# Loading a norm's rows later, and reordering the start of a norm's second tile, in a two-block transformer kernel

## What is computed

```python
x = layer_norm(ALPHA * x + 0.5 * swiglu(x, ffn1_gate[l], ffn1_up[l], ffn1_down[l]), ln1_g[l], ln1_b[l])
proj = x @ w_in[l]
(h_a, b_a, c_a, uv, q, kc, vc, ksl, vsl, kw, vw, gl) = jnp.split(proj, split_points, axis=-1)
y_a = short_conv(h_a, b_a, c_a, conv_w[l])
y_b = gmlp_spatial(uv, ...)
y_c = nsa_attention(q, kc, vc, ksl, vsl, kw, vw, gl, ...)
mix = jnp.concatenate([y_a, y_b, y_c], axis=-1) @ w_out[l]
x = layer_norm(ALPHA * x + mix, ln2_g[l], ln2_b[l])
x = layer_norm(ALPHA * x + 0.5 * swiglu(x, ffn2_gate[l], ffn2_up[l], ffn2_down[l]), ln3_g[l], ln3_b[l])
```

## Time and profile before

| | us |
|---|---|
| timed runs, median of 3 | 2010.58 (2009.91 to 2010.92) |
| profiled execution | 2009.22 |
| its span (first to last instruction) | 2007.4 |
| PE busy | 1980.2 |
| DVE busy | 1263.8 |
| ACT busy | 904.8 |
| POOL busy | 72.8 |

### The profile page before, as it was taken

The page is one execution under the profiler, slowest core; times in us unless marked ns, Lnnn a source line. Parts: engine busy times, 40 slices in busy tenths (PEclk is TensorE's granted clock), DMA queues, the critical chain, the costliest instruction groups (busy, mean ns, idle before and its releaser), DMA issues.

```text
span 2007.4 us, 31808 instructions
## 1 busy us (share of the span) xinstructions
PE 1980.2 (99%) x13856; PEld 1802.3 (90%) x13856; DVE 1263.8 (63%) x1790; ACT 904.8 (45%) x1188; POOL 72.8 (4%) x74
## 2 busy tenths in 40 slices
PE   8999999999999999999999999999999999999998
PEld 7888999999787999999899988799999998879997
DVE  6566666555656665655665567765566556776555
ACT  4445544444445444444344435444435444544442
POOL 0000001000100000100100010010010001001000
PEclk9999999999999999999999999999999999999999
DMA  7544556666543456686576655468657665546663
GB/s 288 168 146 142 181 197 195 206 206 190 175 163 132 166 175 199 189 251 189 168 217 190 187 153 158 106 191 244 189 170 225 186 189 150 149 107 193 189 189 105
DMA packets 421412, 361.84 MB, mean 180 GB/s; under 512 B 29392, under 2 KB 361496, under 8 KB 421272
## 3 DMA queue, kind: packets, MB, share of 16 engines
q1 hardware_dynamic: 421272, 359.80, 58.6%
HBM read 358.72 MB, written 1.05 MB: 179 GB/s over the span
## 4 chain that ended last, share of the span: by engine, by line
PE 89%; DVE 6%; ACT 2%; POOL 1%; DMA 1%; issue 1%; SPq 0%; DVEq 0%; ACTq 0%
PE ps L217 21%; PE ps L218 21%; PE ps L219 21%; PE ps L224 7%; PE ps L226 7%; PE ps L225 7%; PE ps L1488 2%; DVE hl L1997 2%; ACT hl L1776 1%; PE ps L1596 1%; DMA raw<-in_w_in 1%; POOL hl L1952 1%; PE ps L1630 1%; DVE xs L2057 0%; DVE small L2103 0%
## 5 line engine op out<-in xcount | busy, mean ns | idle before, releaser
L1997 DVE TENSOR_TENSOR hl<-raw,hl 128x1024 fp32r<-128x1024 f32 (+1 forms) x537 | 733.7, 1398 | 397.2 <-ACT hl L1776 395.9
L217 PE MATMUL ps<-xt,hl 128*128 128x256 f32 (+1 forms) x2672 | 755.2, 283 | 5.3 <-DVE hl L1997 5.3
L218 PE MATMUL ps<-xt,hl 128*128 128x256 f32 (+1 forms) x2672 | 746.9, 280 | 0.0
L219 PE MATMUL ps<-xt,hl 128*128 128x256 f32 (+1 forms) x2672 | 746.5, 279 | 0.0
L1776 ACT ACTIVATE hl<-raw 128x2048 fp32r<-128x2048 f32 (+1 forms) x323 | 612.3, 1900 | 224.1 <-PE ps L226 159.9
L217 PEld LDWEIGHTS ps<-xt,hl 128*128 128x128 f32 (+1 forms) x2672 | 501.7, 188 | 11.2 <-DVE hl L1997 5.7
L218 PEld LDWEIGHTS ps<-xt,hl 128*128 128x128 f32 (+1 forms) x2672 | 501.8, 188 | 3.1
L219 PEld LDWEIGHTS ps<-xt,hl 128*128 128x128 f32 (+1 forms) x2672 | 501.5, 188 | 0.2
L224 PE MATMUL ps<-hl,o 128*128 128x512 f32 x656 | 261.3, 398 | 0.0
L226 PE MATMUL ps<-hl,o 128*128 128x512 f32 x656 | 258.9, 395 | 0.0
L225 PE MATMUL ps<-hl,o 128*128 128x512 f32 x656 | 258.8, 394 | 0.0
(11 more groups left out here) (197 smaller groups left out, 1552.9 us busy)
## 6 DMA issues: line engine op xcount, KB each, us to landing
raw<-in_w_in SPq DMA_DIRECT2D x83, 1024.0 KB, 5.0
raw<-in_w_ffn_in SPq DMA_DIRECT2D x88, 512.0 KB, 5.1
raw<-in_ffn_gate SPq DMA_DIRECT2D x88, 512.0 KB, 3.9
raw<-in_ffn_up SPq DMA_DIRECT2D x88, 512.0 KB, 5.2
raw<-in_ffn_down SPq DMA_DIRECT2D x44, 1024.0 KB, 5.0
raw<-in_w_ffn_out SPq DMA_DIRECT2D x22, 1024.0 KB, 5.1
raw<-in_w_out SPq DMA_DIRECT2D x24, 512.0 KB, 4.8
raw<-in_w_branch_a SPq DMA_DIRECT2D x8, 1024.0 KB, 5.0
```

What stands on the lines that cost most here:

```text
L217: e.matmul(out, l[0], r[0], start=start, stop=False)
L218: e.matmul(out, l[0], r[1], start=False, stop=False)
L219: return e.matmul(out, l[1], r[0], start=False, stop=stop)
L1997: e.tensor_tensor(lo[:, c], m["raw"][:, k % NRAW, 0:n][:, c], hi[:, c].bitcast(F), ALU.subtract).then_inc(s.low.up(("low", k), *([("low", ...
```

## The change

Three edits. The rows of the second norm in the second block (`ln2_g_2`, `ln2_b_2`) are loaded at the head of `lin_conv` instead of behind the first projection. In a norm that isn't the last, the second tile's first `bn_stats` stands ahead of `split(0)`; the second one and the rest stay behind it. The inner weight unit's high part is made by two ACT instructions of half the width, and POOL's first low half waits for the first of them only. To allow this, `ln_stats` is written for one half of the width at a time, with a wait on the first half's event ahead of the aggregate; events of high parts have a half in their name; and the very first unit's high parts have a step of their own (`lead_high`), which does what it did.

```diff
-    def prep_next(self):
+    def prep_next(self, halves=False):
         tag = self.new()
-        self.add("prep", tag)
+        self.add("prep", tag, halves)
...
-        def begin():
+        def begin(halves=False):
             nonlocal k
             out.append(("load", (k, self.units[k][0])))
-            out.append(("high", (k, self.units[k][1])))
+            for part in ((0, 2), (1, 2)) if halves else ((0, 1),):
+                out.append(("high", (k, self.units[k][1]) + part))
...
-        def stats(i):
-            add("ln_stats", i, acc[i], smalls[i], new)
+        def stats(i, halves=(0, 1)):
+            for c in halves:
+                add("ln_stats", i, c, acc[i][c], smalls[i], new)
+            if 1 not in halves:
+                return
             add("ln_last" if final else "ln_norm", i, acc[i], smalls[i], rows, new)
             PB.give(*acc[i])
...
-        low = P.prep_next()
+        low = P.prep_next(True)
         turn(0)
         tail[3]()
         for _ in range(2):
             low(2, "pool_low")
+        stats(1, (0,))
         split(0)
-        stats(1)
+        stats(1, (1,))
...
         def lin_conv():
+            rows_in(I["ln2_g_2"][l], I["ln2_b_2"][l], [RT.take() for _ in range(2)] + [Place(m["sg"][:, 1, c * 512:(c + 1) * 512], ("merge split", 1)) for c in range(2)])
             yield from t_parts(*t_proj(w_in, 0))
...
         uv = P.res
-        rows_in(I["ln2_g_2"][l], I["ln2_b_2"][l], [RT.take() for _ in range(2)] + [Place(m["sg"][:, 1, c * 512:(c + 1) * 512], ("merge split", 1)) for c in range(2)])
...
+    def high(k, n, h, parts):
+        c = slice(h * n // parts, (h + 1) * n // parts)
         e.wait_ge(*T["raw", k])
         e.wait_ge(*T["used", k - NHL] if k >= NHL else (None, 0))
-        e.activation(m["hl"][:, k % NHL, 0, 0:n], m["raw"][:, k % NRAW, 0:n], ACT.Copy).then_inc(s.high.up(("high", k)), 1)
+        e.activation(m["hl"][:, k % NHL, 0, c], m["raw"][:, k % NRAW, c], ACT.Copy).then_inc(
+            s.high.up(*([("high", k, h)] if parts == 2 else [("high", k, 0), ("high", k, 1)])), 1)
...
     def pool_low(k, n, h, parts):
-        e.wait_ge(*T["high", k])
+        e.wait_ge(*T["high", k, h])
...
-    def bn(acc, small, event):
+    def ln_stats(i, c, acc, small, v):
         st, mv = small[0:2]
-        for c in range(2):
-            e.wait_ge(*T[acc[c].full])
-            e.bn_stats(st[:, 6 * c:6 * c + 6], acc[c].ap).then_inc(done.up(), 1)
+        e.wait_ge(*T[acc.full])
+        e.bn_stats(st[:, 6 * c:6 * c + 6], acc.ap).then_inc(done.up(("stats", v, i, c)), 1)
+        if not c:
+            return
+        e.wait_ge(*T["stats", v, i, 0])
         e.wait_ge(*done.now)
         e.bn_aggr(mv, st).then_inc(done.up(), 1)
```

More of the change, by code:

```diff
@@ L412, in settled @@
                 for h in range(2):
-                    out.append(("high", (0, self.units[0][1], h)))
+                    out.append(("lead_high", (self.units[0][1], h)))
                     out.append(("low", (0, self.units[0][1], h, 2)))
@@ L417, in settled @@
                 if k < len(self.units):
-                    low[args[0]] = [begin(), 0]
+                    low[args[0]] = [begin(args[1]), 0]
             elif kind == "prep_low":
@@ L1766, in scalar_engine, with lead_high @@
     done = s.act
[L1768 to L1773, removed]
+    def lead_high(n, h):
+        c = slice(h * n // 2, (h + 1) * n // 2)
+        e.wait_ge(*T["lead", h])
+        e.activation(m["hl"][:, 0, 0, c], m["raw"][:, 0, c], ACT.Copy).then_inc(s.high.up(("high", 0, h)), 1)
+    def high(k, n, h, parts):
+        c = slice(h * n // parts, (h + 1) * n // parts)
         e.wait_ge(*T["raw", k])
         e.wait_ge(*T["used", k - NHL] if k >= NHL else (None, 0))
-        e.activation(m["hl"][:, k % NHL, 0, 0:n], m["raw"][:, k % NRAW, 0:n], ACT.Copy).then_inc(s.high.up(("high", k)), 1)
+        e.activation(m["hl"][:, k % NHL, 0, c], m["raw"][:, k % NRAW, c], ACT.Copy).then_inc(
+            s.high.up(*([("high", k, h)] if parts == 2 else [("high", k, 0), ("high", k, 1)])), 1)
     def turn_split(b, blocks, events, taken, dst, before, out, scale):
@@ L1929, in cmp_exp @@
         e.activation(er.ap[:, 0:120], er.ap[:, 0:120], ACT.Exp).then_inc(done.up(("cmp exp", l, i)), 1)
-    run(steps, dict(high=high, turn_split=turn_split, o_split=turn_split, turn_copy=turn_copy, copy=copy, silu_gate=silu_gate, ln_split=ln_split,
+    run(steps, dict(lead_high=lead_high, high=high, turn_split=turn_split, o_split=turn_split, turn_copy=turn_copy, copy=copy, silu_gate=silu_gate, ln_split=ln_split,
                     seed=seed, ffn_gate=ffn_gate, ffn_turn=ffn_turn, ffn_split=ffn_split, soft=soft, biased=biased,
@@ L1950, in pool_low @@
         c = slice(h * n // parts, (h + 1) * n // parts)
-        e.wait_ge(*T["high", k])
+        e.wait_ge(*T["high", k, h])
         e.tensor_tensor(lo[:, c], P.m["raw"][:, k % NRAW, 0:n][:, c], hi[:, c].bitcast(F), ALU.subtract).then_inc(
             s.pool_low.up(("low", k), ("low", k, h)), 1)
-    def ln_stats(i, acc, small, v):
+    def ln_stats(i, c, acc, small, v):
+        if not c:
+            return
         e.wait_ge(*T["mhalf"])
@@ L1995, in low @@
         c = slice(h * n // parts, (h + 1) * n // parts)
-        e.wait_ge(*(T["high", k] if k else T["lead high", h]))
+        e.wait_ge(*T["high", k, h if parts == 2 else 1])
         e.tensor_tensor(lo[:, c], m["raw"][:, k % NRAW, 0:n][:, c], hi[:, c].bitcast(F), ALU.subtract).then_inc(
@@ L2045, in bn @@
         e.wait_ge(*done.now)
-        e.tensor_scalar(mv[:, 1:2], mv[:, 1:2], EPS / ALPHA ** 2, None, ALU.add).then_inc(done.up(event), 1)
-    def ln_stats(i, acc, small, v):
-        bn(acc, small, ("mv", v, i))
+        e.tensor_scalar(mv[:, 1:2], mv[:, 1:2], EPS / ALPHA ** 2, None, ALU.add).then_inc(done.up(("mv", v, i)), 1)
     def ln_norm(i, acc, small, rows, v, out="xn"):
```

## The result

| kernel | median of the timed runs, us | from, to (runs) | profiled execution, us (its span) | mean granted clock |
|---|---|---|---|---|
| before | 2010.23 | 2008.19, 2013.13 (14) | 2009.22 (2007.4) | 0.998 |
| after | 2015.32 | 2014.23, 2015.79 (14) | 2015.7 (2013.8) | 0.995 |

After stands to before as 1.0024, 95% interval 1.0015 to 1.0032: slower by about 5 us, where 8 us faster was forecast.

What follows compares the result with a forecast made beforehand. TensorE, busy for 99% of the span, bounds the kernel, so only its waits pay: 5.3 + 1.5 + 1.15 - 0.2 = 7.8 us, so 2001.4 us profiled; timed 2002.4, own range 2000.8 to 2004, 8 in 10 2000.5 to 2016.

Steps and rivals of the forecast that it cites:

- the term for the norms behind an FFN: Five norms behind an FFN: neither edit is ahead of the first tile's second pass, so gaps of 0.23 us stay; gain 0.
- rival 1: Norms behind an FFN: POOL, starting earlier, holds the second pass's second half; five stalls, 11 us, some 2013.7 us; chance 0.38.
- the two "halves": Rival 1's split: few low clocks, within 0.2% of before (part of 0.20); the other half, slower by more, 0.24.
- The first part: Second block's input projections: moving the row loads lets `lin_k`'s load leave 13.5 us earlier; stalls 5.33, low clock 1.5, together 6.8 us.
- Row loads at no cost: In `lin_conv`: the four moved loads delay nothing, put at 0; if cover were gone, up to 8.8 us.
- Behind mixing parts: Four norms behind a mixing projection: POOL and DVE finish earlier, PE gaps of 0.28 to 0.30 us close; gain 1.15 us.
- The added wait: One more DVE wait in each tile's statistics, twenty at 0.04 us, six on PE's path: 0 to 0.24, taken as 0.2 us.
- The low clock: Behind rival 1's stalls: 1.5 us more for each that a low clock follows; one or two make 2015 to 2017 us.
- Rivals 2 and 3: Projection: half of each stall returns as another wait, about 2005 us (0.09); or stalls stay, only 1 us won, 2009.5 (0.05).

Runs made afterwards that it cites:

- The fifth experiment: The changed kernel, high part still in halves everywhere, but POOL's first low part waits for both halves; 2001.49 us, ratio 0.9950 to the kernel before.
- the sixth: The changed kernel with POOL's low part in four instructions of 512 columns instead of two of 1024; 2003.67 us, ratio 0.9962 to before.
- the seventh: The changed kernel with the first tile's second pass as one DVE instruction of 1024 columns where rows lie in one buffer; 2000.29 us, ratio 0.9945 to before.
- the third experiment: The kernel before with only the second tile's first statistics ahead of the first tile's split, and the added wait; 2012.41 us, ratio 1.0001.
- the first experiment: The kernel before with only the rows' loads moved; 2001.98 us, ratio 0.9953.
- the second experiment: The kernel before with only the inner unit's high part in halves, POOL waiting for the half it reads; 2027.57 us, ratio 1.0076.
- experiment 4: The changed kernel with the high part in halves only in the four norms behind a mixing part; 1998.07 us, ratio 0.9936 to before.

## Why the prediction was wrong

**The step that failed is the term for the norms behind an FFN, which the forecast put at nothing ("the five gaps of 0.23 stay", gain 0), and with it the choice of the forecast (0.48) over rival 1 (0.38).** The runs showed 10.9 us there for the stalls and the longer first gaps, and some 6 us more for the low clock behind them. Rival 1 is what happens, at the place, by the mechanism and nearly at the price that it was given: a half of the second pass some 2.9 us long (2.84), PE idle for 2.2 us (2.10) ahead of the second four blocks, five times, and 2015 to 2017 us with low clocks behind the stalls (2015.32). (By its own figures, 2.4 us from 502.45 against a start at 502.5, the second half would have been 2.35 us late and not 2.2; and the two "halves" into which the chances divide rival 1 are 0.14 and 0.24.) The fifth experiment shows that POOL's start is the cause, the sixth that the hold is as long as one POOL instruction, the seventh that it needs a boundary between two DVE instructions.

**What was weighed badly.** Behind an FFN the forecast argued by what precedes the pass ("neither edit is ahead of that", gain 0). That is true of the first tile's waits and says nothing about an engine that is made to start beside it. (Nor does it cover the second tile: the earlier statistics gain 0.9 us there over the five norms, by the third experiment.) Against the rival it held that no row shows a DVE instruction made longer by POOL. The only row in which the two met had a POOL operation of one column, which could not have shown it: a row that can't show an effect is no evidence against it, and the text said so and yet counted it. What it could show, it showed: POOL gets in between two DVE instructions that follow at once, and POOL and DVE exclude each other. With POOL's start worked out at 0.42 us behind the pass's (measured 0.35) and the halves 0.7 us apart, the rival should have been the likeliest.

The Trainium skill, SBUF — State Buffer, Who interferes with whom, says that a DVE instruction with two SBUF inputs contends with a GpSimd instruction that reads SBUF, that the pair of ports is held exclusively, and that issue order decides who blocks. Here the trace agrees in both directions: 0.75 us became 2.84 for DVE, 4.76 became 5.55 for POOL's pair. The order was settled anew at each instruction here: in the code no wait stands between the two halves of the pass, and DVE's second half still came behind POOL.

**The first part** was right: the SP wait gone, the weight load out early, no stall, no low clock there. The term was 5.3 + 1.5 = 6.8 us; the spans of before and of the first experiment differ by 7.0. The timed medians differ by more, 8.9 us. Kernels that keep the projection stalls scatter (before by 5.4 us, the third experiment by 6.2, the second by 5.5), and those without by 1.3 to 2.3 (15, 10 and 4 runs against 4, 5 or 14); that fits stalls which the low clock follows in some executions and not in others. The mean granted clock of the timed runs fits it too: of the runs of before beside the experiments, those under 2010 us have 0.998 or 0.999, those over 2012 us 0.996 or 0.997, and 0.002 of 2007 us is 4 us. But where the clock was low was seen in one execution of each kernel alone, so this is argued and not shown.

**Row loads at no cost**: right. They leave from 1225.85 on, nothing waits for them, and the first experiment shows it alone.

**Behind mixing parts** the mechanism was right and the term too small: 1.15 us forecast, 2.3 in the account. In three of the four norms the pass is early enough that its second half no longer paces the transposes (1.07 us instead of 1.32 for eight): 3 x 0.25 more, 1.9 in all. Some 0.4 us I could not place. What was missed: a gap ahead of a group is only the visible part when the group itself is paced by the same producer. The third experiment adds that the statistics alone are worth nothing there, and in the second, where the halves are alone, the gaps are still 0.10 to 0.12 us: the two edits are needed together.

**The added wait** was put at 0.04 us by the nearest row, at most 0.24 in all; it costs 0.07 on each of five norms (0.23 to 0.30), 0.35. The bound was too tight: the row it came from was one engine's wait for another, and this is an engine's wait for an event of its own.

**The low clock** behind the stalls was allowed for as one or two stretches of 1.5 us; there were five, of 1.2 to 1.6. Five at the rival's own 1.5 us would have made 2009.22 - 7.8 + 11 + 7.5 = 2019.9 us for the profiled execution, which took 2015.7. So it is in part luck that the time came out within the rival's 2015 to 2017: the rest was made up by larger gains behind the mixing parts (1.2 us more), the gain in the second tiles (1.2), a start that was 1.0 us quicker, and low clocks that cost 0.6 less in all.

**Rivals 2 and 3** are out: no new wait of PE in the projection, and the first part did what it says.

## What to carry to other kernels

When an edit makes GpSimd start earlier, look at what DVE does at that moment: if that is a run of short instructions with two SBUF inputs on the path to PE, GpSimd can get in at the first boundary and hold the next one for a whole instruction of its own, as here. Either keep the early start for places where DVE has room (experiment 4), make the GpSimd instructions short (6), or make the DVE step one instruction (7); an edit shared by several call sites can gain at one and lose at the other. And a lack of rows against a mechanism counts only if a row exists that could have shown it.

## What the runs showed of the hardware

- DVE and POOL alternated by instruction where both read two tensors from SBUF: in the changed kernel the pass's first half, POOL's first low part, the pass's second half, POOL's second low part. DVE's instruction went from 0.75 to 2.84 us beside a POOL instruction of 1024 columns, and to 1.76 beside one of 512.
- A wait of DVE on an event that DVE itself raised earlier cost 0.07 us in a dependent chain (PE's gap behind it 0.30 instead of 0.23 us, five times; gone without the wait).
- Of stalls of PE in otherwise dense work, those of 1.02 us (five) and 0.83 us (five) were followed by no low clock; those of 2.10 us by a granted clock of 0.5 to 0.7, read over the next 3.5 us, in all ten cases (the changed kernel and the second experiment). But of the stalls in the projection, one of 2.82 us in before and one of 3.46 us in the third experiment were followed by 1.00, others of 2.51 and 3.17 us at the same place of the next layer by 0.53 and 0.50, and both of the second experiment, 2.94 and 3.29 us, by 0.53 and 0.50. So the length of a stall alone doesn't decide it, and what does stays open.
